# Sample inputs loaded during the prompt's attention, sample values computed in the tail, and the last sample sequence in fp32

## The chip, the cores and the metric

The kernel runs on one core of one Trainium2 chip. The metric is the device time of one execution in microseconds (us); lower is better. Three runs of the kernel before gave 2239.61, 2245.3 and 2246.15 us, median 2245.3 us.

## The reference, cut to what matters

One layer of a decoder is computed for a prompt of 1024 new rows (plus 16 meta rows) and for 8 running sample sequences with 8 new tokens each and 4096 past positions in 32 pages of 128. The part around the change is the latent attention of the sample sequences, the product of its result with `w_uv`, and the merge with the MLP:

```python
def mla_keys(c_kv, k_r, w_uk, ...):
    k_nope = einsum('...tr,rhd->...thd', c_kv, w_uk)        # r = 256, h = 8, d = 64
    return rms_norm(concat([k_nope, broadcast(k_r)]), gains)

def one_seq(pt, qi, ci, kri):                               # 8 sequences
    c_all  = concat([cache_kv_latent[pt].reshape(4096, 256), ci])
    kr_all = concat([cache_k_rope[pt].reshape(4096, 32), kri])
    s   = einsum('qhd,khd->hqk', qi, mla_keys(c_all, kr_all, w_uk, ...)) * SCALE
    p   = softmax(where(mask, s, -inf))
    ctx = einsum('hqk,kr->qhr', p, c_all)
    return einsum('qhr,rhv->qhv', ctx, w_uv)

h = x + (g_pool * pool_out + g_att * attn_out) @ w_o
z = relu(rms_norm(h, g_mlp) @ w_ff1)
y = h + (z * z) @ w_ff2
```

Everything is fp32 in and out.

## The kernel before, in words

The kernel writes its schedule out by hand: each stage is a block with one instruction stream per engine (TensorE, ScalarE, VectorE, GpSimd, and SyncE, which issues DMAs), ordered among each other by semaphores alone. A stage ends with a barrier of all engines, and its buffers and semaphores are released there (`stage_allocator`). The stages are `front`, `prompt_attention`, `sample_attention`, `sample_values` and `tail`.

Most products keep fp32 accuracy in three passes (`three_pass`, lines 103 to 105): each operand is split into a rounded high part (a copy on ScalarE) and a low part (a subtraction, mostly on VectorE), and TensorE multiplies high by high, high by low and low by high. Products with plain fp32 operands are used where they are few.

`prompt_attention` runs over 16 units `u`: 8 heads `h` with two chunks of 512 queries each. In each unit SyncE loads the next head (for each first chunk) and the next unit's gates (line 884), waits for the mixed result (`S["m"]`, written on VectorE at line 980) and stores it (line 909). There are two buffers for gates and two for the result.

`sample_attention` first prepares `w_uk` (transposes L1499, splits L1522 and L1540), folds the queries into it (`qT`, L1510) and clears `qrz` on GpSimd. Its inputs are loaded by SyncE at the start of the block (lines 1145 to 1151), then the pages. A group is `GP` = 4 pages, and a sequence has `GS` = 8 groups. `NG` = 64 groups go through a ring of `RING` = 16, each with eight DMAs (lines 1141 and 1143). A step `g` transposes the pages of group g (L1245) and multiplies those of group g - 1 with keys and queries (`page`, L103 to L105). Group g - 12 (`LAG`) gets its context product (`context`, L1202 and L1206). For that the pages are split (`ch` by ScalarE L1326, `cl` by GpSimd L1484, in the last steps by VectorE L1386), and so are the probabilities (`prob_hl`, L1446 and L1361). For each sequence the maximum is found (L1266, L1279, `gmax` L1334), subtracted on GpSimd in four pieces (L1479), and the exponential is taken (L1302). The context's two halves are folded by a product (`craw`, L1406 and L1251) and divided by the sum (L1379 and L1381). After the last group is loaded, 13 steps without loads follow (`NG` to `NG + LAG`).

`sample_values` turns the context (L1607, copied by L1622), multiplies it with `w_uv` (L1614) and applies the gates `gs` (L1625, L1627), which gives `m8`, the sample columns of the merged input. SyncE also loads the first four rows of `m` and of `w_o` for the tail here (`ahead`, line 1600), and the block ends only when they have landed.

`tail` multiplies `m` with `w_o` (rows split by L1948 and L1974, weights by L1953 and L1976), in the order k = 0 to 7, and for each k over eight tiles of 128 rows into the eight banks of PSUM. `x` is loaded by GpSimd into the same buffer (line 1735). After that come the norm and the MLP, which has most of the span.

## Time and profile before

| | |
|---|---|
| median of three runs | 2245.3 us (2239.61 to 2246.15) |
| the profiled execution | 2248.1 us |
| its span (first to last instruction) | 2246.3 us |
| mean granted TensorE clock | 0.965 |
| TensorE busy | 2105.4 us (94%) |
| VectorE, ScalarE, GpSimd busy | 1180.2, 820.1, 388.9 us |
| prompt attention | 455.0 to 694.2 us |
| sample attention | 694.2 to 1348.1 us |
| sample values, to the tail's first product | 1348.1 to 1369.0 us |
| DMA | 152.91 MB, 68 GB/s on average |

The profile is of one execution. PE is TensorE, PEld its weight loads, DVE is VectorE, ACT ScalarE, POOL GpSimd and SPq the queue of SyncE, in which DMAs are issued. A busy share is that of the time in which at least one instruction runs; the granted clock 1.00 is 2.4 GHz and 0.50 is 1.2 GHz. In a timeline a bracket tells how long the engine was idle before the instruction and what released it. An fp32 matmul appears as two instructions.

### The profile page before, as it was taken

Reading aid. Unit: us, or ns where it says so; the run is one execution under the profiler, and the core shown is the slowest. Engines: PE = TensorE matmul, PEld = TensorE weight load, DVE = VectorE, ACT = ScalarE, POOL = GpSimd, SP = SyncE. Lnnn points to the kernel's source line nnn. Section 1 sums busy time; section 2 is a strip of 40 time slices with the busy share of each in tenths; the row PEclk is TensorE's granted clock in tenths of the full one; section 3 lists DMA queues with packets and bytes.
Section 4 is the critical chain, followed back from the end, with each engine's and each line's share of the span. In section 5 each row is a group of like instructions: output and inputs, shape, how many; then the busy total and the mean of one; then the engine's idle time right before and its main releaser. Section 6 shows DMA issues by size and latency. Waiting matters only on the chain. (4 is left out here: it accounts for less than half of the span.)

```text
span 2246.3 us, 36495 instructions
## 1 busy us (share of the span) xinstructions
PE 2105.4 (94%) x12667; PEld 1936.4 (86%) x12667; DVE 1180.2 (53%) x2364; ACT 820.1 (37%) x1591; POOL 388.9 (17%) x448
## 2 busy tenths in 40 slices
PE   6998999979987999999999967999999999999998
PEld 5878999868886999999999956889898999999897
DVE  4763311156764777666666654454445444444444
ACT  4552211145553566655656543231122111221111
POOL 1110000023441144444535521000000000000000
PEclk9999999989997999999999987999999999999999
DMA  4232222132223322222222108021111111111102
GB/s 150 82 97 69 58 88 78 55 110 90 85 75 87 86 75 62 69 62 63 63 63 65 38 0 286 1 76 38 38 55 38 56 37 37 37 56 44 49 19 85
DMA packets 146212, 152.91 MB, mean 68 GB/s; under 512 B 50694, under 2 KB 122102, under 8 KB 145021
## 3 DMA queue, kind: packets, MB, share of 16 engines
q1 hardware_dynamic: 140325, 128.28, 19.2%
q0 software_dynamic: 5728, 22.65, 3.2%
q8 instruction: 82, 1.34, 0.3%
q14 instruction: 77, 0.63, 0.1%
HBM read 124.77 MB, written 25.97 MB: 67 GB/s over the span
## 5 line engine op out<-in xcount | busy, mean ns | idle before, releaser
L103 PE MATMUL ps<-mh,f_w1h 128*128 128x384 f32 (+1 forms) x768 | 250.8, 327 | 0.0
L105 PE MATMUL ps<-mh,f_w1l 128*128 128x384 f32 (+1 forms) x768 | 250.7, 326 | 0.0
L104 PE MATMUL ps<-ml,f_w1h 128*128 128x384 f32 (+1 forms) x768 | 250.5, 326 | 0.0
L1291 ACT ACTIVATE sq<-ps 128x512 f32<-128x512 f32 x256 | 153.0, 598 | 235.4 <-PE ps L105 235.4
L1862 ACT ACTIVATE room<-ps 128x384 f32<-128x384 f32 (+1 forms) x96 | 45.5, 474 | 502.1 <-PE ps L105 502.1
L1907 DVE TENSOR_TENSOR t_m<-t_m,ps 128x512 f32<-128x512 f32 x256 | 171.6, 685 | 106.9 <-PE ps L105 106.9
L104 PE MATMUL ps<-f_late_l,f_late_h 128*128 128x512 f32 x512 | 200.1, 391 | 0.0
L105 PE MATMUL ps<-f_late_h,f_late_l 128*128 128x512 f32 x512 | 199.9, 391 | 0.0
L103 PE MATMUL ps<-f_late_h 128*128 128x512 f32 x512 | 199.4, 390 | 0.0
L1887 DVE TENSOR_TENSOR room<-room 128x384 f32<-128x384 f32 (+1 forms) x96 | 51.5, 536 | 253.7 <-ACT room L1862 253.7
L103 PE MATMUL ps<-wq,cTh 128*128 128x320 f32 x512 | 172.6, 337 | 2.1 <-DVE g_attn_b L1355 2.1
L1357 DVE TENSOR_REDUCE ss<-sq 128x8 f32<-128x512 f32 x256 | 172.8, 675 | 0.0
L105 PE MATMUL ps<-wq,cTl 128*128 128x320 f32 x512 | 160.9, 314 | 0.0
L104 PE MATMUL ps<-wq,cTh 128*128 128x320 f32 x512 | 160.6, 314 | 0.0
L1355 DVE TENSOR_TENSOR g_attn_b<-ps,g_attn_b 128x64 f32<-128x64 f32 x256 | 56.9, 222 | 179.3 <-ACT sq L1291 176.2
L103 PEld LDWEIGHTS ps<-mh,f_w1h 128*128 128x128 f32 x768 | 144.3, 188 | 1.9
L104 PEld LDWEIGHTS ps<-ml,f_w1h 128*128 128x128 f32 x768 | 144.2, 188 | 1.8
L103 PE MATMUL ps<-w_late,cTh 128*128 128x256 f32 x512 | 145.6, 284 | 0.0
L105 PE MATMUL ps<-w_late,cTl 128*128 128x256 f32 x512 | 145.5, 284 | 0.0
L104 PE MATMUL ps<-w_late,cTh 128*128 128x256 f32 x512 | 145.4, 284 | 0.0
L105 PEld LDWEIGHTS ps<-mh,f_w1l 128*128 128x128 f32 x768 | 144.2, 188 | 0.0
L1484 POOL TENSOR_TENSOR cl<-c_ring,ch 128x1024 fp32r<-128x1024 f32 x53 | 120.8, 2278 | 22.6 <-ACT ch L1326 22.6
(333 smaller groups left out, 5069.3 us busy)
## 6 DMA issues: line engine op xcount, KB each, us to landing
c_ring<-in_cache_kv_latent SPq DMA_DIRECT2D x256, 128.0 KB, 2.0
f_raw<-in_w_ff SPq DMA_DIRECT2D x32, 1024.0 KB, 5.3
m_raw<-in_w_in SPq DMA_DIRECT2D x20, 512.0 KB, 3.9
gated<-gate POOLq DMA_DIRECT2D x8, 1088.0 KB, 5.2
pa_gm<-gated SPq DMA_DIRECT2D x16, 512.0 KB, 4.9
fr_x<-in_x_prompt SPq DMA_DIRECT2D x8, 512.0 KB, 3.6
mixed<-pa_mixed SPq DMA_DIRECT2D x16, 256.0 KB, 2.1
kr_ring<-in_cache_k_rope SPq DMA_DIRECT2D x256, 16.0 KB, 1.8
```

What stands on the lines that cost most here:

```text
L103: nc.tensor.matmul(out, lh, rh, start=first, stop=False)
L104: nc.tensor.matmul(out, lh, rl, start=False, stop=False)
L105: return nc.tensor.matmul(out, ll, rh, start=False, stop=last)
L1291: nc.scalar.activation(sq[:, j % 2, :].rearrange("p (a n) -> p a n", a=2), ps[:, kn_bank(j):kn_bank(j) + 2, 0:HALF], ACT.Square).then_inc( ...
L1355: nc.vector.tensor_tensor(summed[:, p1, j * HQ:(j + 1) * HQ], ps[:, kn_bank(j), HALF:HALF + HQ], rope[:, p1, j * HQ:(j + 1) * HQ], ALU.add ...
L1357: nc.vector.tensor_reduce(ss[:, p1, j * H:(j + 1) * H], sq[:, j % 2, :].rearrange("p (h d) -> p h d", d=NOPE), AX.X, ALU.add).then_inc(S[" ...
L1484: nc.gpsimd.tensor_tensor(cl[:, (k - LAG + 1) % 2, :, 0:KV], c_ring[:, (k - LAG + 1) % RING, :, :], f32(ch[:, (k - LAG + 1) % 2, :, 0:KV]) ...
L1862: nc.scalar.activation(z[:, a, 0:w], ps[:, 2 * par + a, 0:w], ACT.Relu).then_inc(S["relu"], 1)
L1887: nc.vector.tensor_tensor(z[:, a, 0:w], z[:, a, 0:w], z[:, a, 0:w], ALU.mult).then_inc(S["z"], 1)
L1907: nc.vector.tensor_tensor(part, part, ps[:, bank, :], ALU.add).then_inc(S["y"], 1)
```

## The change

The inputs of the sample stage (`w_uk`, the sample queries and keys, `c_new`) are loaded by SyncE in unit 2 of the prompt's attention, and the first four groups of pages (`EARLY`) one each in units 3 to 6, ahead of that unit's wait for its result. For this the sample stage's buffers are all allocated at the start of the program (`sample_tiles`), and the clearing of `c_new` moves to GpSimd's stream in the prompt's attention.

In the last sequence the maximum is subtracted on VectorE. Its probabilities and pages are not split: 33 fp32 products take the place of the eight split context steps, VectorE sums the probabilities, and four small products with ones add the sums over the rows. The steps after the last load are 5 in place of 13.

`sample_values` is gone. Its products come first in the tail's TensorE stream. `w_uv` and the gates are loaded behind the tail's first rows, ScalarE copies the turned context, and VectorE applies the gates behind its splits for k = 0. `x` for the sample tile and the gain for the norm are loaded later. The rows of `m` and `w_o` are no longer loaded ahead of the block.

```diff
+EARLY = 4
...
+            nc.gpsimd.memset(B["c_new"][:, 0:KV], 0.0).then_inc(arrived["zeros"], 1)
+            nc.gpsimd.memset(B["c_new"][:, KV:KV + 1], 1.0)
...
+
+                if u == 2:
+                    sample_inputs(nc, A, C, B, arrived, Q, c_rows)
+                if 3 <= u < 3 + EARLY:
+                    k = u - 3
+                    load_pages(nc, A, C, B["c_early"][:, k], B["kr_ring"][:, k], arrived["groups"][k], k)
                 sp.wait_ge(S["m"], u + 1)
...
+        sb("room", [P, NSEQ * KV])
...
+        sb("wq", [P, 2, 2, 2, HALF + HQ], F32R)
...
+        sb("c_ring", [P, RING - EARLY, GP, KV])
...
+        sb("c_new", [P, KV + 1])
+        sb("kr_ring", [P, GS, GP, ROPE])
+        sb("c_early", [P, EARLY, GP, KV])
+
+    early = B["prob"][:].rearrange("p a t n -> p (a t n)")
+    B["w_uk"] = early[:, 0:2 * H * NOPE].rearrange("p (k n) -> p k n", k=2)
...
+def sample_inputs(nc, A, C, B, arrived, Q, c_rows):
+    sp = nc.sync
+    sp.dma_start(B["w_uk"], A["w_uk"].rearrange("(k p) h d -> p k (h d)", p=P)).then_inc(arrived["uk"], 16)
+    sp.dma_start(B["qT"], Q[0][:, :, 0:TS]).then_inc(arrived["qk"], 16)
+    sp.dma_start(B["kT"], Q[1][:, :, 0:TS]).then_inc(arrived["qk"], 16)
+    for j in range(GP):
+        sp.dma_start(B["qr"][ROPE * j:ROPE * (j + 1)], Q[0][NOPE:QK, :, 0:TS]).then_inc(arrived["qr"], 16)
+    sp.wait_ge(arrived["zeros"], 1)
+    sp.dma_start(B["c_new"][0:TS, 0:KV], c_rows).then_inc(arrived["rows"], 16)
+def load_pages(nc, A, C, c_tile, kr_tile, arrived, g):
+    cache, krope = A["cache_kv_latent"], A["cache_k_rope"]
+    for j in range(GP):
+        page = nc.sync.value_load(C["pages"][0:1, bass.ds(g * GP + j, 1)], min_val=0, max_val=cache.shape[0] - 1)
+        nc.sync.dma_start(c_tile[:, j, :], cache[bass.ds(page, 1), :, :].rearrange("a p n -> p (a n)")).then_inc(arrived, 16)
+        nc.sync.dma_start(kr_tile[:, j, :], krope[bass.ds(page, 1), :, :].rearrange("a p n -> p (a n)")).then_inc(arrived, 16)
...
+        c_ring = [B["c_early"][:, k] for k in range(EARLY)] + [B["c_ring"][:, k] for k in range(RING - EARLY)]
...
-            sp.dma_start(w_uk, A["w_uk"].rearrange("(k p) h d -> p k (h d)", p=P)).then_inc(uk_in, 16)
-            sp.dma_start(qT, Q[0][:, :, 0:TS]).then_inc(qk_in, 16)
-            sp.dma_start(kT, Q[1][:, :, 0:TS]).then_inc(qk_in, 16)
-            for j in range(GP):
-                sp.dma_start(qr[ROPE * j:ROPE * (j + 1)], Q[0][NOPE:QK, :, 0:TS]).then_inc(qr_in, 16)
-            sp.wait_ge(S["zeros"], 1)
-            sp.dma_start(B["c_new"][0:TS, 0:KV], c_rows).then_inc(rows_in, 16)
-            for k in range(RING):
+                load_pages(nc, A, C, c_ring[k], kr_ring[:, k % GS], group_in[k], g)
+            for k in range(EARLY, RING):
...
-                for g in range(NG, NG + LAG + 1):
+                for g in range(NG, NG + 5):
...
+        def split_context(g, back, valid, loading):
+
+            return valid(back) and (loading or g - back < NG - GS)
...
-            if valid(LAG):
+            if split_context(g, LAG, valid, loading):
                 context()
...
-            split = last_of(k, 5, valid)
+            split = loading and last_of(k, 5, valid)
...
+            if not loading and last_of(k, 4, valid):
+                b = seq_of(lap, k, 4)
+                par = ((k - 4) % RING) // GS
+                dve.wait_ge(S["gmax"], b + 1)
+                dve.wait_ge(S["newcopied"], b + 1)
+                for i in range(NP):
+                    span = slice(parts[i].start, parts[i].stop + (i == NP - 1))
+                    piece = prob[:, par, span, :]
+                    nc.vector.tensor_tensor(piece, piece,
+                                            gmax[:, par, :].unsqueeze(1).broadcast_to([P, span.stop - span.start, HQ]),
+                                            ALU.subtract).then_inc(S["shifted"], 1)
...
-            if last_of(k, 5, valid):
+            if loading and last_of(k, 5, valid):
...
-            if last_of(k, 4, valid):
+            if loading and last_of(k, 4, valid):
...
+            end = (NSEQ - 1) * NP
+            for i in range(NP):
+                pe.wait_ge(S["exp"], end + i + 1)
+                for t in range(parts[i].start, parts[i].stop):
+                    nc.tensor.matmul(ps[0:HQ, 3, 0:KV], prob[:, 1, t, :], c_ring[GS + t // GP][:, t % GP, :], start=t == 0, stop=False)
+            last = nc.tensor.matmul(ps[0:HQ, 3, 0:KV], prob[:, 1, NPAGE, :], B["c_new"][:, 0:KV], start=False, stop=True)
+            pe.wait_ge(S["sums"], NP)
+            for i in range(NP):
+                last = nc.tensor.matmul(ps[0:HQ, 4, 0:HQ], most[:, i, :], ones[:], start=i == 0, stop=i == NP - 1)
+            last.then_inc(S["end"], 1)
...
+            end = NSEQ - 1
+            for i in range(NP):
+                span = slice(parts[i].start, parts[i].stop + (i == NP - 1))
+                dve.wait_ge(S["exp"], end * NP + i + 1)
+                nc.vector.tensor_reduce(most[:, i, :], prob[:, 1, span, :].rearrange("p t n -> p n t"), AX.X, ALU.add
+                                        ).then_inc(S["sums"], 1)
+            dve.wait_ge(S["end"], 1)
+            nc.vector.reciprocal(rden[:, end:end + 1], ps[0:HQ, 4, 0:1]).then_inc(S["rden"], 1)
+            dve.wait_ge(S["rden"], NSEQ)
+            nc.vector.tensor_scalar(ctxs[:, end, :], ps[0:HQ, 3, 0:KV], rden[:, end:end + 1], None, ALU.mult)
...
-            nc.gpsimd.memset(B["c_new"][:], 0.0).then_inc(S["zeros"], 1)
...
-def sample_values(nc, A, C, ps, ctxs, G, m8, ahead):
...
+        ctxT = h8[:].rearrange("p (c b h q) -> p c b h q", c=2, b=NSEQ, h=H)
+        gs = gain[:].rearrange("p (w h n) -> p w h n", w=2, h=H)
...
-            for k in range(4, KD):
-                sp.dma_start(m[:, k, :], m_rows[k]).then_inc(m_in[k - 4], 16)
-            for i in range(4, 2 * KD):
+            for i in range(2 * KD):
                 half, k = i // KD, i % KD
-                sp.wait_ge(S["wol"], i - 3)
+                if i < KD:
+                    sp.dma_start(m[:, i, :], m_rows[i]).then_inc(m_in[i], 16)
+                if i >= 4:
+                    sp.wait_ge(S["wol"], i - 3)
                 sp.dma_start(o_raw[:, i % 4, :], w_o[:, k, 512 * half:512 * half + 512]).then_inc(in_o[i % 4], 16)
-                if i == 4:
+                if i == 0:
+                    sp.dma_start(raw2[:], A["w_uv"].rearrange("(k p) h d -> p k (h d)", p=P)).then_inc(uv_in, 16)
+                    for w in range(2):
+                        sp.dma_start(gs[:, w], G[:, :, w, SEQ:TOK].rearrange("j p n -> p j n")).then_inc(gates_in, 16)
+                if i == KD:
+                    sp.wait_ge(S["m8"], 1)
...
-            nc.gpsimd.memset(h8[TS:P, :], 0.0).then_inc(S["h8z"], 1)
-            pool.dma_start(h8[0:TS, :], x_tiles[8]).then_inc(x_in[8], 16)
             for t in range(8):
                 pool.wait_ge(S["ml"], t + 1)
                 pool.dma_start(h[t], x_tiles[t]).then_inc(x_in[t], 16)
+            pool.wait_ge(S["values"], 1)
+            nc.gpsimd.memset(h8[TS:P, :], 0.0).then_inc(S["h8z"], 1)
+            pool.dma_start(h8[0:TS, :], x_tiles[8]).then_inc(x_in[8], 16)
...
+            for rc in range(2):
+                for b in range(NSEQ):
+                    last = nc.tensor.transpose(ps[:, 5 + rc, b * TS:(b + 1) * TS], ctxs[:, b, rc * P:(rc + 1) * P],
+                                               C["ident"][0:TS, 0:TS])
+                last.then_inc(S["ctx_turned"], 1)
+            pe.wait_ge(uv_in, 16)
+            pe.wait_ge(S["ctx_copied"], 2)
+            for j in range(H):
+                for rc in range(2):
+                    last = nc.tensor.matmul(ps[:, 7, j * TS:(j + 1) * TS], raw2[:, rc, j * VH:(j + 1) * VH],
+                                            ctxT[:, rc, :, j, :], start=rc == 0, stop=rc == 1)
+            last.then_inc(S["values"], 1)
...
+                    if k == 0 and n == 7:
+                        pe.wait_ge(S["gated"], 1)
...
+                if k == 0:
+                    dve.wait_ge(S["values"], 1)
+                    dve.wait_ge(gates_in, 32)
+                    nc.vector.tensor_tensor(m8[:], ps[:, 7, :].rearrange("p (h n) -> p h n", h=H), gs[:, 1], ALU.mult
+                                            ).then_inc(S["gated"], 1)
+                    dve.wait_ge(S["gated"], 1)
+                    nc.vector.tensor_tensor(m8[:], m8[:], gs[:, 0], ALU.add).then_inc(S["m8"], 1)
...
+            prompt_attention(nc, A, C, ps, cTh, cTl, Q, G, m, B, arrived, c_rows)
+
+        sample_attention(nc, A, C, ps, B, arrived)
```

## Rows read from the trace of the kernel before

**Rows 1.** The page: busy us, share of span and instructions by engine.

```profile
PE 2105.4 (94%) x12667; PEld 1936.4 (86%) x12667; DVE 1180.2 (53%) x2364; ACT 820.1 (37%) x1591; POOL 388.9 (17%) x448
```

**Rows 2.** Windows: length, busy time by engine (instructions), granted clock, DMA share, GB/s.

```profile
694.24:714.92 20.68, 12.88 (x76) 11.00 (x76) 10.93 (x23) 7.01 (x13) 5.86 (x8) 0.58 0.48 119
...
1310.00:1348.14 38.14, 20.53 (x102) 15.32 (x99) 21.07 (x32) 15.14 (x18) 9.67 (x14) 0.72 0.00 0
...
1348.14:1369.02 20.88, 9.00 (x48) 8.68 (x48) 4.65 (x7) 2.97 (x5) 1.84 (x3) 0.50 0.81 262
```

**Rows 3.** Timeline, TensorE, start of sample stage: start, duration, operation [idle before].

```profile
697.96 3.62 PE L1499 MATMUL ps<-ident,prob 128*64 128x128 f32 x16 [8.26 <-DMA prob<-in_w_uk]
...
708.26 1.94 PE L1245 MATMUL ps<-ident,c_ring 128*128 128x128 f32 x8 [0.53 <-DMA kr_ring<-in_cache_k_rope]
...
714.92 1.97 PE L1245 MATMUL ps<-ident,c_ring 128*128 128x128 f32 x8 [1.21 <-DMA kr_ring<-in_cache_k_rope]
...
716.54 0.61 PE L103 MATMUL ps<-wq,cTh 128*128 128x320 f32 x1
```

**Rows 4.** Timeline, SyncE's transfers, prompt attention and start of the sample stage.

```profile
514.75 0.53 SPq L884 DMA_DIRECT2D pa_gm<-gated  x1
...
519.97 0.34 SPq L909 DMA_DIRECT2D mixed<-pa_mixed  x1
...
571.27 0.53 SPq L884 DMA_DIRECT2D pa_gm<-gated  x1
...
576.22 0.34 SPq L909 DMA_DIRECT2D mixed<-pa_mixed  x1
...
694.24 0.38 SPq L1145 DMA_DIRECT2D prob<-in_w_uk  x1
...
698.79 0.61 SPq L1151 DMA_DIRECT2D c_new<-c_rows  x1
...
700.70 0.38 SPq L1141 DMA_DIRECT2D c_ring<-in_cache_kv_latent  x1
...
707.23 0.34 SPq L1141 DMA_DIRECT2D c_ring<-in_cache_kv_latent  x1
```

**Rows 5.** Timeline, all engines, end of the sample stage.

```profile
1318.97 0.22 ACT L1334 ACTIVATE gmax<-ps 128x64 f32<-128x64 f32 x1 [4.69 <-PE ps L1279]
...
1319.27 6.06 POOL L1479 TENSOR_TENSOR prob<-prob,gmax 128x512 f32<-128x512 f32 x4 [3.53 <-ACT gmax L1334]
...
1320.16 1.28 ACT L1302 ACT_TABLE_LOAD   x1
...
1322.41 1.12 PE L1251 MATMUL ps<-craw,fold 128*64 128x257 f32 x2 [0.52 <-DVE craw L1406]
...
1329.87 0.58 PE L1202 MATMUL ps<-ch,prob_hl 128*128 128x258 f32 x1 [6.34 <-DVE prob_hl L1361]
...
1345.58 0.65 PE L1251 MATMUL ps<-craw,fold 128*64 128x257 f32 x2 [0.52 <-DVE craw L1406]
...
1346.45 0.47 DVE L1381 TENSOR_SCALAR room<-ps,rden 64x256 f32<-64x256 f32 x1
```

**Rows 6.** Timeline, TensorE, values stage and first product of the tail.

```profile
1354.14 7.06 PE L1614 MATMUL ps<-ctxT,s_w_uv 128*128 128x64 f32 x32 [4.03 <-DMA s_w_uv<-in_w_uv]
...
1369.02 0.79 PE L103 MATMUL ps<-f_w1h,mh 128*128 128x512 f32 x1 [7.82 <-DVE f_w1l L1976]
```

**Rows 7.** Timeline, TensorE, twelve instructions of six fp32 matmuls in the front.

```profile
58.49 4.04 PE L668 MATMUL ps<-fr_w_uq,fr_qlT 128*128 128x384 f32 x12
```

**Rows 8.** One line's VectorE instructions: minimum/median/maximum ns, first and last start.

```profile
L1361 DVE TENSOR_TENSOR prob_hl<-prob,prob_hl x32: 675/682/2621, 809.6 to 1330.9; 128x512 fp32r<-128x512 f32 x32
```

**Rows 9.** Windows of 2 us, columns as in Rows 2.

```profile
718.00:720.00 2.00, 2.00 (x12) 2.00 (x12) 0.84 (x2) 0.33 (x2) 0.00 (x0) 0.66 0.34 82
...
1332.00:1334.00 2.00, 1.68 (x8) 1.38 (x6) 0.92 (x1) 1.34 (x2) 0.00 (x0) 0.56 0.00 0
...
1374.00:1376.00 2.00, 2.00 (x9) 1.61 (x8) 1.31 (x2) 0.00 (x0) 0.79 (x2) 0.82 1.02 404
```

More of the change, by code:

```diff
@@ L1064, in _, with sample_tiles, sb @@
                     last.then_inc(S["pv"], 1)
-def sample_attention(nc, A, C, ps, Q, c_rows, ctxs):
+def sample_tiles(nc, C):
+    HQ = H * NNEW
+    HALF = H // 2 * NOPE
+    B = {}
+    with ExitStack() as ctx:
+        def sb(name, shape, dt=F32):
+            B[name] = ctx.enter_context(nc.sbuf_tensor(name, list(shape), dt))
+        sb("room", [P, NSEQ * KV])
+        sb("wq", [P, 2, 2, 2, HALF + HQ], F32R)
+        sb("w_late", [P, 2, 2, HALF], F32R)
+        sb("qt", [P, NSEQ, 2, 2, HQ], F32R)
+        sb("qrz", [P, NSEQ, 2, GP, HQ], F32R)
+        sb("s_new", [P, NSEQ, HQ])
+        sb("fold", [P, HQ])
+        sb("new_mask", [TS, NSEQ, NNEW])
+        sb("c_ring", [P, RING - EARLY, GP, KV])
+        sb("cTh", [P, 2, 2, GP * PAGE], F32R)
+        sb("cTl", [P, 2, 2, GP * PAGE], F32R)
+        sb("krTh", [P, 2, PAGE], F32R)
+        sb("krTl", [P, 2, PAGE], F32R)
+        sb("sq", [P, 2, H * NOPE])
+        sb("krsq", [P, 2, GP, ROPE])
+        for name in ("ss", "var", "sd", "rinv"):
+            sb(name, [P, 2, GP * H])
+        sb("krss", [P, 2, GP])
+        sb("most", [P, GP, HQ])
+        sb("lmax", [P, 2, HQ])
+        sb("gmax", [P, 2, HQ])
+        sb("top", [HQ, 1])
+        sb("eps", [P, 1])
+        sb("turn", [1, 4])
+        sb("rden", [HQ, NSEQ])
+        sb("sa_ones", [P, HQ])
+        sb("ch", [P, 2, GP, KV + 2], F32R)
+        sb("cl", [P, 2, GP, KV + 2], F32R)
+        sb("craw", [P, KV + 1])
+        sb("prob_hl", [P, NPAGE, 2, HQ], F32R)
+        sb("prob", [P, 2, NPAGE + 1, HQ])
+        sb("c_new", [P, KV + 1])
[3 more added lines that the diff above has]
+    B["w_uk"] = early[:, 0:2 * H * NOPE].rearrange("p (k n) -> p k n", k=2)
+    B["w_ukT"] = early[0:NOPE, 1024:1024 + H * KV].rearrange("p (h r) -> p h r", h=H)
+    for name, a in (("qT", 3072), ("kT", 3584)):
+        B[name] = early[0:QK, a:a + H * TS].rearrange("p (h n) -> p h n", h=H)
+    B["qr"] = C["g_attn"][:, 2 * GP * HQ:2 * GP * HQ + H * TS].rearrange("p (h n) -> p h n", h=H)
+    B["rope"] = C["g_attn"][:, 0:2 * GP * HQ].rearrange("p (a n) -> p a n", a=2)
+    B["summed"] = C["g_attn"][:, 2 * GP * HQ:4 * GP * HQ].rearrange("p (a n) -> p a n", a=2)
+    return B
@@ new lines, in sample_attention @@
+        sq, krsq, krss, ss, var, sd, rinv = (B[name] for name in ("sq", "krsq", "krss", "ss", "var", "sd", "rinv"))
+        prob, prob_hl, rope, summed = (B[name] for name in ("prob", "prob_hl", "rope", "summed"))
+        most, lmax, gmax, top, eps, turn, rden = (B[name] for name in ("most", "lmax", "gmax", "top", "eps", "turn", "rden"))
+        ch, cl, craw, mask, ones = (B[name] for name in ("ch", "cl", "craw", "new_mask", "sa_ones"))
+        w_uk, w_ukT, qT, kT, qr = (B[name] for name in ("w_uk", "w_ukT", "qT", "kT", "qr"))
@@ L1121, in sample_attention @@
+        uk_in, qk_in, qr_in, rows_in = (arrived[name] for name in ("uk", "qk", "qr", "rows"))
+        group_in = arrived["groups"]
         S = {k: sem("sa_" + k) for k in (
@@ L1632, in tail_pieces, with tail @@
-def tail_pieces(A, sb, m):
-    T = {"m": sb("t_m", [P, H, SEQ]), "raw1": sb("f_raw1", [P, KD, FB])}
-    o_raw = T["raw1"][:].rearrange("p k f -> p (k f)").rearrange("p (a n) -> p a n", a=4)
-    w_o = A["w_o"].rearrange("(k p) n -> p k n", p=P)
-    ahead = []
-    for i in range(4):
-        ahead += [(T["m"][:, i, :], m[i]), (o_raw[:, i, :], w_o[:, i, 0:512])]
-    return T, ahead
-def tail(nc, A, C, ps, T, room, m_rows, m8, x_tiles, results):
+def tail(nc, A, C, ps, room, ctxs, m_rows, G, x_tiles, results):
@@ L1942, in _ @@
         def _(act):
+            for rc in range(2):
+                act.wait_ge(S["ctx_turned"], rc + 1)
+                nc.scalar.activation(ctxT[:, rc].rearrange("p b h q -> p (b h q)"), ps[:, 5 + rc, :], ACT.Copy
+                                     ).then_inc(S["ctx_copied"], 1)
             for i in range(2 * KD):
@@ L2035, in program @@
             tiles.append(([(0, P, xp[t])], P, 1 + t, P * t, TS + a, [(0, P, y["c_p"][0, a:a + P, :], y["kr_p"][0, a:a + P, :])]))
+        B = sample_tiles(nc, C)
+        arrived = {k: nc.alloc_semaphore("sa_in_" + k) for k in ("uk", "qk", "qr", "rows", "zeros")}
+        arrived["groups"] = [nc.alloc_semaphore(f"group_in{k}") for k in range(RING)]
         with ExitStack() as prompt:
```

139 lines of the change are left out of this document (26 added, 113 removed).

## The prediction

> **What bounds the kernel now.** I read the page first: TensorE is busy for 2105.4 of 2246.3 us [rows 1]. A change that takes work from another engine, or moves a transfer, can therefore win only where TensorE itself stands still or waits at half clock. All of the change lies around three such places, which the windows by stage show [rows 2]. At the start of the sample stage (694.24 to 714.92) TensorE is busy for 12.88 of 20.68 us. At its end (1310 to 1348.14) it is busy for 20.53 of 38.14 us. In the values stage and up to the tail's first product (1348.14 to 1369.02) it is busy for 9.00 of 20.88 us. That is some 37 us of idleness, part of it waits that the change does not touch.
>
> Then I read the timeline of each place for what ends the waits. At the start TensorE waits 8.26 us until `w_uk` has landed, later 0.53 us for the first group of pages and 1.21 us for the second [rows 3]. At the end, GpSimd's four subtractions of the maximum take 6.06 us, and TensorE then stands for 6.34 us until the split probabilities are there [rows 5]. After that it follows the splitting of the pages, group by group, until the fold at 1345.58 and the scaling that ends at 1346.92 [rows 5]. In the values stage it waits 4.03 us for `w_uv`, works 7.06 us, and waits 7.82 us more for the tail's first operands [rows 6].
>
> **Part 1: inputs and four groups of pages moved into the prompt's attention.** The three waits above for DMAs go. The block before still ends at 694.24, since its last store does not move. The transposes of `w_uk` then start at about 694.3 in place of 697.96, which gives 3.66 us; the two waits for pages give 0.53 + 1.21 us. Together 5.4 us [rows 3]. The steps in between (ScalarE and VectorE splits of `w_uk`, `qT` products) keep their offsets from that start, as all hang on it. GpSimd's clearing of `qrz` does not move earlier, but its users come late enough.
>
> Against that stands the clock. In the window 718 to 720 the mean granted clock is 0.66; with the levels 1.2 and 2.4 GHz (0.5 and 1) the rise lies at 719.4, 2.8 us after dense products begin at 716.54 [rows 3, 9]. After two other restarts (1329.87 and 1369.02) the windows with 0.56 and 0.82 put it at 1333.8 and 1374.7 in the same way, that is 3.9 and 5.7 us later [rows 5, 6, 9]. The new start comes at another moment, so I expect 2.8 to 5.7 us at half clock and take 4.8: 2 us more, of which half is lost. The gain is 4.4 us, between 3 and 5.5.
>
> What it costs SyncE: `sample_inputs` issues eight transfers in 5.2 us (694.24 to 699.40), and a group's eight take 6.5 us (700.70 to 707.23) [rows 4]. In unit 2 SyncE has 4.7 us between the end of the gates' issue and the store of `mixed`, in unit 6 it has 4.4 us [rows 4]. So one or two stores of `mixed` and the loads of gates behind them go out 0.5 to 2 us late. Nothing on TensorE waits for them: the buffer is taken again two units on, and the gates are used at a unit's end. I cost this at nothing. Without that cover the price is all of SyncE's added time, 5.2 + 4 x 6.5 = 31 us. GpSimd's two small memsets come ahead of work that waits for a transfer anyway.
>
> **Part 2: the last sequence in fp32.** It removes eight steps with their page splits on ScalarE and VectorE, the casts on GpSimd and the splits of the probabilities. Up to the fold of the sequence before, at 1322.41, nothing changes. VectorE now subtracts the maximum: it may start at 1319.2 [rows 5], and four operations of 0.68 us [rows 8] end at 1321.9. So `craw`, which is queued behind them, is not held up, and the fold runs as before, until 1323.5. The four exponentials, of which the first can end by 1322.1 (behind the table load at 1320.16 [rows 5]), lie beside it. TensorE goes straight on from 1323.5, so the 6.34 us wait is gone.
>
> What comes in its place is 32 + 1 fp32 products of 256 columns. Six such products of 384 columns took 4.04 us at full clock [rows 7]: 1.75 ns a column with the pipeline's end, so 0.43 us for 256 columns and 0.86 at half clock. If 4.5 us of the run are at half clock, five products fall there, and 28 x 0.43 = 12.0 us follow: 16.5 us, the end is at 1340.0. The sums' four small products with VectorE's reciprocal and scaling: old fold to old end is 1345.58 to 1346.92, 1.34 us [rows 5]; I take 1.5. The stage's work ends at 1341.5 in place of 1346.92: **5.4 us**. Bounds: all at full clock 33 x 0.43 = 14.2 us, gain 7.7; all at half clock 28.4 us, a loss of 6.5.
>
> A rule of the Trainium skill speaks against this part ("FP8 and Floating Point Precision", section "TensorE Precision Notes"): true fp32 takes four passes through the array. The high and low products that go take two. Here the trace agrees: 384 columns at 2.4 GHz are 0.16 us, and a product took 0.67 [rows 7]. If TensorE's passes set the time of this stretch, two more passes of 256 columns for 32 pages would cost 6.8 us. They don't set it before, as the waits in [rows 5] show.
>
> **Part 3: sample values in the tail.** One stage goes, with its barrier and its wait for eight prefetched transfers. In the tail the order of TensorE is transposes, values, products. Take T0 = 1342.7 (the end plus 1.2 us of block change, as from 1346.92 to 1348.14). `w_uv` is now the third transfer, behind one row of `m` and one of `w_o`, 0.79 MB. Alone it needed 6.0 us from 1348.14 to 1354.14 [rows 6]; 0.79 MB at 262 GB/s [rows 2] are 3.0 us. The values' products start at T0 + 9.0, take 7.06 us at half clock, and the tail's products start at T0 + 16.2 = 1358.9. Before, this was 20.88 us [rows 2], so **4.7 us** are gained. Bounds: with full clock for the values 3.5 us more; with `w_uv` landing only with the whole batch, as below, 3 us lost.
>
> Beside other work: VectorE is queued behind the values before it splits k = 1, but then splits a row and a weight in about 1.9 us, where TensorE needs 24 x 0.23 = 5.4 us for each k. The gate products add 1.4 us on VectorE under k = 0. The last x tile and the gain are later on GpSimd and SyncE but are used only some 40 us on.
>
> **Sum.** 4.4 + 5.4 + 4.7 = 14.5 us. The span goes from 2246.3 to 2231.8, the profiled execution from 2248.1 to 2233.6. The median of the runs shown, 2245.3, is 2.8 us below that execution, so I forecast 2231. A measurement of this kernel can tell about 0.3%, 6.7 us.
>
> **The rivals.**
> A. The clock stays at 1.2 GHz for the whole fp32 run. The values' products stayed there for 7.06 dense us (the clock of the window is 0.50) [rows 2, 6], but they stream only 64 columns per weight load, these 256. Part 2 loses 6.5: total 2.6, **2243**, no change.
> B. The transfers share the queue, and `w_uv` lands with the batch it is issued in, some 17 us after T0. Part 3 becomes a loss of 3 to 4 us: total about 6.5, **2239**.
> C. The early inputs save only the two waits for pages, since ScalarE's and GpSimd's steps in the setup bound it. Then 3.7 us less: **2235**.
> D. TensorE keeps 2.4 GHz through the fp32 run and the values: 2.3 + 3.5 us more, **2225**. That TensorE works from the fold at 1322.41 on almost without a gap speaks for it, the wait for `w_uv` against. The skill ("TensorE: Matmul & The Clock Gate", "Part 4: PE-mode transpose") says that transposes don't hold the clock up, so by it the 16 transposes don't bridge that wait; in this trace the window from 1348.14, which begins with such transposes, has 0.50 throughout [rows 2].
> E. The other sign: SyncE's added issues push loads of gates and heads onto the path of the prompt's attention. Up to 31 us come back, **2262**. It decides from 21 us on (14.5 + 6.7), so nearly all must show. The gaps of 4.4 to 4.7 us before the stores, and 6.5 us per group, speak for some delay; that nothing waits soon for what is delayed speaks against it.
> That the change does less than it says is A and C.
>
> **How the numbers follow.** My forecast 0.65; A 0.08, B 0.07, C 0.10, D 0.07, E 0.03. Forecast's own range: part 1 from 3 to 5.5, part 2 from 4 to 7.5, part 3 from 2.5 to 7, so 2225.5 to 2236. With B and C, and half of A's way, the range is 2224 to 2240. Faster by over 0.3%: 0.63 of the forecast, C, D and a part of B, 0.83. Within 0.3%: A, the rest of B, a little of the forecast, 0.13. Slower: E and a sum of A and B, 0.04.
>
> **What would show it.** Part 1: the first TensorE instruction of the sample stage follows the barrier at once, and the second group's transposes come about 5.4 us sooner after it. Part 2: from the fold to the last scaling about 19 us, with no idle time on TensorE, and the fp32 products at 0.21 us spacing per instruction after a few at 0.43. Part 3: from block change to first product about 16 us, most of the first 9 idle. The sample stage begins at 694.2 as now. Wrong: a later begin of it, a run of fp32 products at half clock to the end, or a wait of over 10 us for `w_uv`.

## The result, and the profile after

The changed kernel takes 2224.16 us, the median of five runs (2218.99 to 2230.93), against 2245.3 us of the kernel before (2239.61 to 2246.24). The ratio is 0.9917 [0.9902, 0.9932], a gain of 21.1 us. The forecast was 2231, so the gain is 6.6 us larger than the 14.5 worked out: 2224.16 lies at the lower edge of the stated range (2224 to 2240) and below the 2225.5 to 2236 of the forecast itself. Two later sets of runs gave 0.9925 [0.9907, 0.9944] and 0.991 [0.9896, 0.9923], gains of 17.1 and 20.3 us.

The page of the changed kernel, its part on busy time, stands against [rows 1]. TensorE's work hardly falls; its span falls by 24.1 us.

```profile
span 2222.2 us, 36454 instructions
...
PE 2101.2 (95%) x12673; PEld 1929.6 (87%) x12673; DVE 1172.5 (53%) x2358; ACT 813.6 (37%) x1585; POOL 379.8 (17%) x436
```

The windows of the changed kernel, columns as in [rows 2]: from the start of the sample stage to the second group's transposes, one sequence boundary inside the stage (used further down), the run of fp32 products, and the values up to the tail's first product.

```profile
693.64:709.05 15.41, 12.81 (x76) 11.29 (x77) 10.93 (x24) 6.62 (x12) 5.38 (x7) 0.61 0.30 80
1027.27:1038.76 11.49, 9.65 (x73) 8.93 (x72) 9.46 (x21) 7.22 (x13) 10.24 (x13) 1.00 0.22 54
...
1312.96:1327.20 14.24, 14.24 (x67) 9.04 (x66) 4.50 (x6) 0.00 (x0) 0.00 (x0) 1.00 0.00 0
1329.60:1345.37 15.77, 8.02 (x48) 7.92 (x49) 1.83 (x2) 4.27 (x6) 0.62 (x1) 0.60 0.94 297
```

The first stretch took 20.68 us before [rows 2] and takes 15.41 now, with the same 12.8 to 12.9 us of work in it. The fp32 run has no gap at all: 14.24 us busy out of 14.24, at a granted clock of 1.00.

TensorE's timeline at the start of the sample stage, against [rows 3]. The waits for DMAs are gone; what is left is the block change (4.57 us) and two waits for VectorE (0.25 us, not shown, and 2.30 us).

```profile
693.68 3.59 PE L1561 MATMUL ps<-ident,prob 128*64 128x128 f32 x16 [4.57 <-PEq L793]
...
703.76 1.97 PE L1296 MATMUL ps<-ident,c_early 128*128 128x128 f32 x8
...
708.24 0.58 PE L104 MATMUL ps<-qrz,krTh 128*128 128x256 f32 x1 [2.30 <-DVE krTl L1458]
...
709.05 1.91 PE L1296 MATMUL ps<-ident,c_early 128*128 128x128 f32 x8
710.61 0.61 PE L104 MATMUL ps<-wq,cTh 128*128 128x320 f32 x1
711.02 0.47 PE L105 MATMUL ps<-wq,cTh 128*128 128x320 f32 x1
711.29 0.43 PE L106 MATMUL ps<-wq,cTl 128*128 128x320 f32 x1
711.56 0.29 PE L104 MATMUL ps<-w_late,cTh 128*128 128x256 f32 x1
711.68 0.28 PE L105 MATMUL ps<-w_late,cTh 128*128 128x256 f32 x1
```

The begins show the clock: 0.27 us from one product of 320 columns to the next up to 711.56, then 0.12 us between products of 256. TensorE got 2.4 GHz at 711.6, 0.95 us after the first product with 320 columns (710.61). Before it was 2.8 us after [rows 3, 9]. Counted from the end of TensorE's last idle time the two are closer, 3.3 us here (from 708.24) and 4.5 us before (from 714.92), since the wait of 1.21 us ahead of the transposes is gone.

TensorE's timeline at the end of the sample stage and in the values, against [rows 5, 6]:

```profile
1312.48 0.65 PE L1302 MATMUL ps<-craw,fold 128*64 128x257 f32 x2 [0.52 <-DVE craw L1468]
1312.96 13.98 PE L1582 MATMUL ps<-c_ring,prob 128*64 128x256 f32 x64
1326.78 0.59 PE L1583 MATMUL ps<-c_new,prob 128*64 128x256 f32 x2
1327.21 0.63 PE L1586 MATMUL ps<-sa_ones,most 128*64 128x64 f32 x8
...
1338.53 7.09 PE L1958 MATMUL ps<-h,f_raw 128*128 128x64 f32 x32 [7.70 <-DMA f_raw<-in_w_uv]
1345.37 0.77 PE L104 MATMUL ps<-f_w1h,mh 128*128 128x512 f32 x1
```

The same stretch on VectorE. Its subtractions, four in 2.56 us against GpSimd's 6.06 [rows 5], end at 1311.86, and the last scaling ends the stage's work at 1328.55.

```profile
1309.30 2.56 DVE L1447 TENSOR_TENSOR prob<-prob,gmax 128x512 f32<-128x512 f32 x4 [1.03 <-ACT gmax L1385]
1312.00 0.43 DVE L1468 COPY craw<-ps 128x257 f32<-128x257 f32 x1
...
1328.07 0.48 DVE L1642 TENSOR_SCALAR room<-ps,rden 64x256 f32<-64x256 f32 x1
```

**Where the 24.1 us of the two spans come from.** I measured from marker to marker, so that each stretch stands alone (times in us; before, after, difference):

| stretch | before | after | gain |
|---|---|---|---|
| begin of the sample stage | 694.24 | 693.64 | 0.6 |
| from there to the second group's transposes | 20.68 | 15.41 | 5.3 |
| second to third group | 9.80 | 8.93 | 0.9 |
| third group (724.72, 717.98) to the last (1291.67, 1280.16) | 566.95 | 562.18 | 4.8 |
| last group to the end of the last scaling | 55.25 | 48.39 | 6.9 |
| from there to the tail's first product | 22.10 | 16.82 | 5.3 |
| the rest of the tail | 877.28 | 876.83 | 0.4 |

The fourth row is the surprise. The change touches nothing there, and it holds a fifth of the difference. The experiments have to tell whether that is the change's.

### The profile page after: what moved, and what is told of

Its sections match the earlier page's. It is cut to its first block and busy times, and to the rows that moved or that the text cites. A ratio compares the mean times of both kernels' runs of the same rounds, so it can differ in the third digit from the quotient of the medians.

```text
span 2222.2 us, 36454 instructions
## 1 busy us (share of the span) xinstructions
PE 2101.2 (95%) x12673; PEld 1929.6 (87%) x12673; DVE 1172.5 (53%) x2358; ACT 813.6 (37%) x1585; POOL 379.8 (17%) x436
## 5 line engine op out<-in xcount | busy, mean ns | idle before, releaser
L1894 ACT ACTIVATE tail_room<-ps 128x384 f32<-128x384 f32 (+1 forms) x96 | 45.5, 474 | 502.1 <-PE ps L106 502.1
L1919 DVE TENSOR_TENSOR tail_room<-tail_room 128x384 f32<-128x384 f32 (+1 forms) x96 | 51.5, 536 | 253.7 <-ACT tail_room L1894 253.7
L106 PEld LDWEIGHTS ps<-f_late_h,f_late_l 128*128 128x128 f32 x512 | 96.1, 188 | 20.2
```

The source lines that it names most:

```text
L106: return nc.tensor.matmul(out, ll, rh, start=False, stop=last)
L1894: nc.scalar.activation(z[:, a, 0:w], ps[:, 2 * par + a, 0:w], ACT.Relu).then_inc(S["relu"], 1)
L1919: nc.vector.tensor_tensor(z[:, a, 0:w], z[:, a, 0:w], z[:, a, 0:w], ALU.mult).then_inc(S["z"], 1)
```

## The experiments

Three sets of runs, each beside runs of the kernel before: its median was 2243.69 us (11 runs) in the first, 2242.61 (17) in the second and 2244.53 (9) in the third. The changed kernel was in the first and the third; a kernel of the second set is compared with it across sets, so only to some 2 to 3 us. The kernels of the first set ran six times each, and their means differ less than their medians: against after_again by 3.0 us for part 1, 6.7 for part 2 and 4.2 for part 3, each with a standard error of about 2 us. The sizes below are therefore good to some 4 us where they come from times alone; the profiles show where they arise.

### First set: each part undone alone

**after_again.** The changed kernel once more.

> The changed kernel once more, unaltered, beside the kernel before. My theory of the 21 us: about 6 us from the start of the sample stage, 7 from its end, 5 from the values, and the rest (4.8 us in the profiled pair, between the third and the last group of pages) is not the change's at all but how often TensorE's clock happens to fall between two sequences. Theory: the median is 17 to 23 us under the kernel before, and the stretch from the transposes of the third group to those of the 64th, 562.2 us in the first profile of this kernel and 567.0 in that of the kernel before, comes out at another value between 559 and 568. Rival, that the change makes the loop itself faster: 562.2 again, within 0.5 us.

Measured: 2226.56 us, ratio 0.9925 [0.9907, 0.9944]. Its profile has 565.69 us in the fourth stretch of the table, not 562.18, while the end of the stage (48.39) is as above and the stretch to the tail's first product is 15.91 in place of 16.82.

**late_inputs.** Part 1 undone: the inputs and all pages are loaded in the sample stage.

```diff
-                if u == 2:
-                    sample_inputs(nc, A, C, B, arrived, Q, c_rows)
-                if 3 <= u < 3 + EARLY:
-                    k = u - 3
-                    load_pages(...)
...
-            for k in range(EARLY, RING):
+            sample_inputs(nc, A, C, B, arrived, Q, c_rows)
+            for k in range(RING):
```

> The changed kernel with part 1 undone: all inputs and all groups of pages are loaded in the sample stage again. Theory: waits for DMAs of some 8.3, 0.5 and 1.2 us come back, 5.4 us against the changed kernel, with 1 us more or less from the clock at the restart: 4.5 to 7 us slower than it, so 14 to 17 us faster than the kernel before. Rival, that part 1 also makes the loop faster: 10 to 11 us slower than the changed kernel. Rival, that the setup is bound by GpSimd and ScalarE: under 2 us slower.

Measured: 2231.28 us, ratio 0.9937 [0.9921, 0.9954]; part 1 is worth 4.7 us in the medians. That is 12.4 us faster than the kernel before, where at least 14 were expected. TensorE's timeline of this kernel has the three waits of [rows 3] back:

```profile
697.40 3.62 PE L1557 MATMUL ps<-ident,prob 128*64 128x128 f32 x16 [8.07 <-DMA prob<-in_w_uk]
...
707.59 1.94 PE L1292 MATMUL ps<-ident,c_early 128*128 128x128 f32 x8 [0.42 <-DMA kr_ring<-in_cache_k_rope]
```

8.07 us idle in place of 4.57, then 0.42 and 1.27 us for pages: 5.2 us. From the second to the third group it needs 9.81 us, as before, so it lacks the 0.9 us of the clock too. That term is no fixed size, though: in the eleven profiles with part 1 in place this step takes 8.93 to 10.24 us, on average 9.33, and in split_last (9.84) and fp32_twice (10.24) it gains nothing. In the three profiles without part 1 it takes 9.79 to 9.89.

**split_last.** Part 2 undone: the last sequence is split, subtracted on GpSimd, and takes 13 steps.

```diff
-                for g in range(NG, NG + 5):
+                for g in range(NG, NG + LAG + 1):
...
-            return valid(back) and (loading or g - back < NG - GS)
+            return valid(back)
...
-            split = loading and last_of(k, 5, valid)
+            split = last_of(k, 5, valid)
...
```

> The changed kernel with part 2 undone: the last sequence is split as the others, with 13 steps after the last load. Theory: the stretch from the transposes of the last group to the last scaling of the context goes from 48.4 back to 55.3 us, the kernel is 5.5 to 7.5 us slower than the changed one and the wait of 6.3 us for the split probabilities is back. Rival, that little of it counts since the clock gives or takes as much: under 3 us slower.

Measured: 2234.55 us, ratio 0.9957 [0.9941, 0.9974]; part 2 is worth 8.0 us, a little more than the 5.5 to 7.5 expected. From the last group to the last scaling its profile has 56.44 us in place of 48.39, 8.05 more. The chain is the one of before: after the fold TensorE waits 6.33 us for the split probabilities, then for the low parts of the pages. Part 2 holds two steps, the subtraction on VectorE and the products without splits; no run separates them, so what each is worth stays open.

```profile
1312.19 1.12 PE L1302 MATMUL ps<-craw,fold 128*64 128x257 f32 x2 [0.52 <-DVE craw L1457]
1319.64 0.58 PE L1253 MATMUL ps<-ch,prob_hl 128*128 128x258 f32 x1 [6.33 <-DVE prob_hl L1412]
...
1324.23 0.66 PE L1257 MATMUL ps<-cl,prob_hl 128*64 128x258 f32 x4 [1.07 <-DVE cl L1437]
```

**values_apart.** Part 3 undone: the stage `sample_values` with its barrier and its transfers ahead is back.

```diff
+def sample_values(nc, A, C, ps, ctxs, G, m8, ahead):
...
+            for dst, source in ahead:
+                sp.dma_start(dst, source).then_inc(ahead_in, 16)
+            sp.wait_ge(ahead_in, 16 * len(ahead))
```

> The changed kernel with part 3 undone: the sample values have their stage again, with the barrier and the prefetched rows. Theory: from the last scaling of the context to the first product of the tail goes from 16.8 back to 22.1 us, the kernel is 4.5 to 6 us slower than the changed one. Rival, that the rows loaded ahead pay for the stage later in the tail: under 2 us slower.

Measured: 2232.04 us, ratio 0.9943 [0.9924, 0.9963]; part 3 is worth 5.5 us. The stretch from the last scaling to the first product is 21.46 us, against 15.91 of after_again. The three parts sum to 18.2 us, and the whole change gained 17.1 in this set: they add up within the noise, and nothing asks for a fourth part.

### Second set: what the pieces cost now

**fp32_twice.** Each fp32 product of a page is issued twice.

```diff
-                for t in range(parts[i].start, parts[i].stop):
+                for n, t in enumerate([t for t in range(parts[i].start, parts[i].stop) for _again in range(2)]):
...
```

> The changed kernel with each of the 32 fp32 products of the last sequence issued twice (its context is then doubled against the new rows' part, so the sample outputs are not the reference's). In the profile of the changed kernel the 64 instructions took 13.98 us, all at full clock. Theory: TensorE is the bound of that stretch and a product costs 0.43 us, so 13.8 us come on top, between 13 and 15. Rival, that at a run twice as long the clock falls: over 20 us. Rival, that the products lie beside VectorE's sums: under 10 us.

Measured: 2241.71 us, ratio 0.9993 [0.9982, 1.0004]: 15.1 to 17.6 us above the changed kernel's medians in the other sets, and the whole gain of the change is gone. The profile has the run at twice its length (its timeline):

```profile
1316.22 29.31 PE L1582 MATMUL ps<-c_ring,prob 128*64 128x256 f32 x128
```

Values_apart, whose fp32 run begins at the same lower clock (its fold takes 1.12 us too), has 15.38 us for 64 instructions. So the 32 added products cost 13.9 us, 0.44 each, at full price. Nothing else bounds this stretch now: TensorE's products do. The Trainium skill ("FP8 and Floating Point Precision", section "TensorE Precision Notes") gives true fp32 four passes; four times 256 columns at 2.4 GHz are 0.43 us, and the run agrees. It was right to hold this rule against the change, but before it the passes were not what TensorE spent its time on there.

**values_ready.** `w_uv` and the gates are loaded during the last sample steps, `w_uv` into the buffer of the early pages, so the values find their operands.

```diff
+            sp.wait_ge(S["ctx"], NG - LAG)
+            raw2 = B["held"][:, 0:2 * D].rearrange("p (k n) -> p k n", k=2)
+            sp.dma_start(raw2, A["w_uv"]...).then_inc(arrived["uv"], 16)
+            sp.wait_ge(S["scaled"], NG)
...
+                sp.dma_start(gs[:, w], G[...]).then_inc(arrived["gates"], 16)
```

> The changed kernel with w_uv and the gates loaded during the last sequence of the sample stage, into the ring slots that are free by then (c_early is moved up by 3 KB a partition, and the tail's m8, h8 and w_uv buffer are views of it). In the changed kernel TensorE waits 7.7 us in the tail for w_uv. Theory: that wait goes and nothing takes its place, since the tail's first row and weight are split some 6.5 us after its start and the values' products take 7.1 us: the first product of the tail comes some 9 to 10.5 us after the last scaling in place of 15.9 to 16.8, and the kernel is 5.5 to 7 us faster than the changed one. Rival, that the first row's split is the next wait, or that the later rows are late: under 3 us faster.

Measured: 2218.77 us, ratio 0.9894 [0.9881, 0.9908], 5.4 to 7.8 us below the changed kernel's medians. Against the kernel before, beside which it ran, it gains 23.8 us where the changed kernel gained 17.1 to 21.1, so 2.7 to 6.7 us more. In the profile the stretch from the last scaling to the tail's first product is 9.88 us in place of 15.91 to 16.82, within the 9 to 10.5 expected. TensorE's timeline of the values:

```profile
1332.84 1.18 PE L1957 MATMUL ps<-ident,room 64*128 64x64 f32 x16 [1.82 <-PEq L1170]
1334.80 7.06 PE L1964 MATMUL ps<-c_early 128*128 128x64 f32 x32 [0.78 <-ACT c_early L1997]
1341.62 0.77 PE L104 MATMUL ps<-f_w1h,mh 128*128 128x512 f32 x1
```

And the windows of the turning of the context and of the values, where the column after POOL's busy time is the granted clock:

```profile
1332.80:1334.80 2.00, 1.18 (x16) 1.10 (x17) 0.00 (x0) 1.10 (x2) 0.00 (x0) 0.95 0.51 164
1334.80:1341.62 6.82, 6.82 (x33) 6.82 (x33) 1.83 (x2) 1.76 (x3) 0.63 (x1) 0.50 0.87 305
```

The 7.70 us wait (6.77 and 6.96 in the two other profiles of the changed kernel) is now 0.78. The values still take 7.06 us at 1.2 GHz, although they come straight behind a stretch at 0.95: the long wait for `w_uv` isn't needed to put them at half clock. So rival D's second half does not come about even with its obstacle gone. Whether the two short idle times left, 1.82 and 0.78 us around the turning, have a part in it was not tried.

**two_groups.** Two early groups in place of four.

```diff
-                if 3 <= u < 3 + EARLY:
+                if 3 <= u < 5:
...
-            for k in range(EARLY, RING):
+            for k in range(2, RING):
```

> The changed kernel with only two of the four groups of pages loaded early. The kernel before waited for the first two groups alone. Theory: the third group is wanted some 24 us after the block begins and is loaded in 6.5 us, so the time is that of the changed kernel within 1.5 us. Rival, that all four early groups count: 2 us slower or more.

Measured: 2224.7 us, ratio 0.9913 [0.9901, 0.9926], a gain of 17.9 us, as the changed kernel. No DMA ends a wait of TensorE between 690 and 800 us. The third and fourth early groups buy nothing that shows: the ring's other transfers start at the block's begin and are in time.

**uv_first.** In the tail `w_uv` is the first transfer, not the third.

```diff
+            sp.dma_start(raw2[:], A["w_uv"]...).then_inc(uv_in, 16)
             for i in range(2 * KD):
```

> The changed kernel with w_uv as the first transfer of the tail, ahead of the first row of m and of w_o. Theory: it lands about 6 us after the tail begins in place of 8.9, and the first row and weight land some 3 us later, still under the values' products; 2 to 3 us faster than the changed kernel. Rival, that all transfers share the queue and w_uv lands as late as now: within 1 us of it.

Measured: 2222.34 us, ratio 0.9906 [0.9893, 0.9919]. In the profile the wait falls from between 6.77 and 7.70 us to 4.04 us and the stretch from 16.82, 15.91 and 16.10 in three profiles of the changed kernel to 13.18; the median is 1.8 to 4.2 us lower, but the gain over the kernel before, 20.3 us, is no larger than the changed kernel's 17.1 to 21.1. So the gain is shown by the profile alone. TensorE's timeline:

```profile
1339.58 7.09 PE L1958 MATMUL ps<-h,f_raw 128*128 128x64 f32 x32 [4.04 <-DMA f_raw<-in_w_uv]
```

### Third set: the stretch that the change does not touch

From the first border of two sequences on, most groups follow each other in steps of 8.65 to 8.68 us (one step a sequence takes 9.8 us and one 9.4, in every profile). At the border one step is longer still, where the first context products of the sequence wait for their probabilities. The seven such steps, from the begin of one group's transposes to the next's:

| kernel | us |
|---|---|
| before | 14.37, 11.47, 12.94, 13.02, 12.93, 11.51, 12.95 |
| after | 15.48, 13.00, 12.93, 11.49, 11.41, 11.50, 11.41 |
| after_again | 15.51, 12.99, 12.92, 11.48, 12.94, 11.48, 11.40 |

Behind the first, which takes 14.2 to 15.5 us, a border costs about 11.5 or about 13.0 us, in the same kernel. One of each kind, as windows: of the kernel before the step from 1032.76, and of the changed one that from 1027.27 (shown above with the other windows).

```profile
1032.76:1045.78 13.02, 11.17 (x72) 10.45 (x71) 9.47 (x21) 7.22 (x13) 10.25 (x13) 0.87 0.22 59
```

The other engines' work is the same in both, to 0.01 us; TensorE's is 1.52 us longer at a clock of 0.87 against 1.00. In both TensorE waits for the split probabilities (1.85 and 1.84 us). After some of these waits the clock falls, after others not.

The borders hold only 1.9 of the 4.8 us between the first two profiles. Another 3.4 us lie where the loop over 16 groups turns, ahead of the 33rd and the 49th group (the other steps give 0.5 back). There TensorE is idle for 1.4 to 2.2 us with nothing to wait for in the profile, and the step behind it takes 8.7 to 9.2 us at full clock or 10.3 us with a fall. Both such steps of the kernel before had the fall, none of the changed kernel's first profile; after_again and after_third had one each and before_again none. The first turn, before and after:

```profile
994.66 1.09 PE L1245 MATMUL ps<-ident,c_ring 128*128 128x128 f32 x8 [1.87 <-issue]
990.51 1.09 PE L1296 MATMUL ps<-ident,c_early 128*128 128x128 f32 x8 [1.43 <-issue]
```

And the windows of the two steps, 0.83 and 1.00 being the granted clock:

```profile
994.66:1004.91 10.25, 10.25 (x68) 10.25 (x69) 4.58 (x13) 4.21 (x8) 3.12 (x3) 0.83 0.20 49
990.51:999.36 8.85, 8.85 (x68) 8.77 (x69) 4.91 (x15) 4.20 (x8) 3.01 (x3) 1.00 0.21 55
```

**kept_busy.** Products whose result is overwritten fill the wait at the borders. The wait for `ctxn` moves ahead of them.

```diff
+                if gi == 0:
+                    for _fill in range(14):
+                        nc.tensor.matmul(ps[:, 7, 0:HALF], cTh[:, p1, 0, 0:P], B["w_late"][:, 0, 0, :], start=True, stop=True)
                 if gi % 2 == 0:
                     pe.wait_ge(S["prob_lo"], ...)
```

> The changed kernel with 14 products added before TensorE's wait for each sequence's first split probabilities (their result is overwritten; about 1.5 us at full clock, where it waits 1.85 us). It tests what the clock costs between sequences: in the profile of the kernel before, one such boundary took 13.02 us with a mean granted clock of 0.87, in that of the changed kernel 11.49 us with 1.00, with the same wait. Theory: the short idle time lets the clock fall at some boundaries and not at others. Without it none falls, the stretch from the third to the 64th group's transposes is 554 to 558 us (559.5 to 567.0 in six profiles so far), and the kernel is 3 to 7 us faster than the changed one. Rival, that the clock falls for another reason: the stretch stays above 559 us and the time is the same or up to 3 us longer.

Measured: 2222.37 us, ratio 0.99 [0.9885, 0.9915]. That is only 1.9 us below after_third, which these runs do not tell from nothing: the size is a miss. The mechanism is in the profile. The timeline has the wait at 0.36 us, and all borders but the first (12.87 us) take 11.67 to 11.69:

```profile
1030.34 1.94 PE L1244 MATMUL ps<-w_late,cTh 128*128 128x256 f32 x14 [0.36 <-DVE room L1435]
1032.12 0.28 PE L1256 MATMUL ps<-ch,prob_hl 128*128 128x258 f32 x1
```

A border that would have been slow gains 1.3 us, one that would not loses 0.2. The stretch is 558.31 us, against 562.18, 565.69 and 562.76, so 4 to 7 us are won there in the profiles, 3.0 to 5.8 of them at the borders; the turns of the loop got no added products, and neither has a fall in this profile. What takes most of it back in the median is only partly seen: in this profile the fp32 run begins at half clock, and the end of the stage takes 50.20 us in place of 48.39. TensorE's first work of the sample stage also comes 2.7 us later than in after_third (696.08 for 693.41), which no part of this edit touches.

**ready_and_busy.** values_ready and kept_busy together.

> The same filling products on the kernel that loads w_uv and the gates during the last sequence. Theory: both gains add, 9 to 13 us under the changed kernel, some 2213 us. Rival: one of them alone shows, 2218 us or more.

Measured: 2213.3 us (2212.69 to 2214.16), ratio 0.9861 [0.9846, 0.9876], 10.9 us below after_third and the fastest of all. Its four runs lie within 1.5 us; five of after_third span 4.3. The stretches are 558.01 and 10.30 us.

**before_again, after_third.** Both kernels once more beside these.

> The kernel before once more, unaltered, for its profile. Theory: the stretch between the third and the 64th group's transposes is not 567.0 us again but some other value between 555 and 568; the start of the stage, its end and the values' stage keep their 30.5, 55.3 and 22.1 us within 2 us each. Rival: 567 us again.

> The changed kernel, unaltered, on the chip of these runs, as what the two filled kernels are compared with. 2221 to 2229 us.

Measured: 2240.4 us in a single run, and 2224.23 us, ratio 0.991 [0.9896, 0.9923]. The profile of before_again has 560.57 us in the untouched stretch. The two profiles of the kernel before are 6.4 us apart there, those of the changed kernel lie between them (562.18, 562.76, 565.69). In both profiles of the kernel before the other stretches keep their lengths (the end of the stage 55.25 and 55.13 us, the values 22.10 and 21.92). So nothing shows that the 4.8 us in the table are the change's: two executions of one kernel differ by more, at the borders and at the turns of the loop.

## Why the prediction was right, and where it was off

The three waits and what replaces them came as forecast, each part with its sign. The size was too small, 14.5 us against 17.1 to 21.1. The three medians, 2224.16, 2226.56 and 2224.23, lie within the range but at its lower bound of 2224: that the first does is luck by 0.2 us.

**Part 1** gave 5.3 us up to the second group, where 5.4 was worked out. The clock term had the wrong sign in this profile. I took 4.8 us at half clock after the restart and so a loss of 1.0; it was 0.95 us, and a gain of 0.9. Over the eleven profiles with part 1 the gain is 0.5 us on average, and in one, fp32_twice, it is a loss of 0.4. Together 6.2 us by the two profiles, against 4.4; undoing the part cost 4.7 us in the median. Rival C is out: ScalarE's and VectorE's steps kept their offsets.

**SyncE's cost** was 9.3 us for the inputs, not 5.2. Its issues in unit 2, against [rows 4]:

```profile
517.36 6.55 SPq L1145 DMA_DIRECT2D g_attn_b<-q_rows  x4
523.96 0.61 SPq L1147 DMA_DIRECT2D c_new<-c_rows  x1
524.61 0.58 SPq L918 DMA_DIRECT2D mixed<-pa_mixed  x1
```

The four transfers of query rows take 6.55 us to issue; what holds them was not tried. The store of `mixed` went out at 524.61 in place of 519.97 [rows 4], 4.6 us later and not 0.5 to 2. Of the stores beside the groups' transfers none is more than some 2 us late. All this was still free, as argued. The 0.6 us by which the sample stage begins sooner are scatter, but TensorE's last product ahead of it ends at 688.2 to 691.5 us (on average 689.7) in the eleven profiles with the early transfers and at 688.7 to 689.7 in the three without: rival E's 31 us are out.

**Part 2** is the step whose size was off: forecast 5.4, measured 6.9 between the two profiles and 8.0 by undoing it. The term is "if 4.5 us of the run are at half clock". Measured from the fold, the run and the sums took 16.1 us where I had 19.1, and in the five profiles whose run began at half clock 17.8 to 17.9. Of those 3.0 us the run itself is 2.2, the fold at full clock 0.6 and the sums 0.2. The fp32 products themselves are as priced, 0.43 us each: 13.98 us for 32. (The 1.75 ns a column of [rows 7] would make it 0.45 us; the rounding down was not worked out, and came out right.) The profile shows 6.9 and not 8.4 because TensorE's clock was 0.67 in a stretch ahead of the fold (1293.49 to 1298.49), so the fold came 32.32 us after the last group in place of 30.74. That fall is in 11 of the 12 profiles with a changed kernel or a part of it, split_last among them, and in neither of the two of before. fp32_twice, which has the same code up to the fold, lacks it (30.80). So the code does not compel it; whether the rest is chance or goes back to what the earlier parts moved stays open.

**Part 3**: `w_uv` arrived 8.9 us after the block's begin (1329.60 to 1338.53), 9.0 were forecast; the values took 7.09 us for 7.06; the first product came after 15.8 us for 16.2 (TensorE's need for each k, 24 x 0.23, is 5.5 us and not 5.4, on which nothing hangs). The gain is 5.3 us, 5.5 by undoing it, for 4.7. Rival B is out.

**The rivals.** Of D one half came in this profile: full clock through the fp32 run, worth 2.3 us by my own sum. It came in four of the ten profiles with a run of this length, the three of the changed kernel among them; five began at half clock (15.3 to 15.4 us in place of 13.98) and ready_and_busy lies between (14.09). The other, full clock for the values, did not, and does not in values_ready either. D's sum of 2225 is nearest to the measured time, yet its 3.5 us for the values are not in it. In the two profiles other things stand in their place: 1.9 us of clock in part 1, 0.6 in part 3, and the 4.8 us of the stretch that the change does not touch. A is out: the clock was 1.00 in the whole run, and where it began at 0.50 it rose within it. In the values, with 64 columns in place of 256 for each weight load, it stayed at 0.50.

Summed by measured parts the change is worth 4.7 + 8.0 + 5.5 = 18.2 us, and 17.1 to 21.1 as a whole.

## What to carry to other kernels

Price a change by the places where the bounding engine stands still, each with what ends its wait: at a stall of the splits, plain fp32 products with twice the passes cost less than the wait they replace, though every one of them is paid in full once the stall is gone. Load what a stage's first instructions need while the stage before still works, and only that much: here two groups did what four did, and loading the next transfer of the kind, `w_uv`, ahead shortened its stretch by another 6.0 to 6.9 us in the profiles. When two profiles differ in a stretch that the edit does not touch, take a second profile of each kernel before explaining it; undoing the parts one by one tells which of them count, and with each such kernel's profile the sizes hold even where the times alone are uncertain by some 4 us.

## What the runs showed of the hardware

The same wait of 1.84 or 1.85 us of TensorE is followed by a fall of its clock in some sequences and not in others, within one execution; each fall costs 1.5 us. The same holds for the idle 1.4 to 2.2 us where the loop turns: 2.00 us without a fall in kept_busy, 1.87 us with one in the kernel before. Filling the wait at the borders with 14 unused products left no fall there in two profiles (11.67 to 11.69 us for each border behind the first). The four runs of ready_and_busy lie within 1.5 us, but those of kept_busy, with the same products, span 4.4, so that the filling steadies the time is not shown.

The values' 16 fp32 products, 128 by 128 weights with 64 columns each, run without a gap for 7.06 to 7.09 us and stay at 1.2 GHz (granted clock 0.50) in all fourteen profiles, even right behind a stretch at 0.95. The tail's products behind them begin at that clock too.
